# Sample rows, forget gates and first loads issued in another form in a two-layer decoder step

## The reference

```python
proj = h @ w_in                       # GLA: q, k, v, g, z; FoX: q, g
k = rms_norm(p[..., :D_B].reshape(B, L, H_B, HD_B)) * k_norm
v = p[..., D_B:2 * D_B].reshape(B, L, H_B, HD_B)
logf = jax.nn.log_sigmoid((p[..., 2 * D_B:] + b_f).astype(jnp.float32))     # 16 heads
f_all = jnp.cumsum(jnp.concatenate([logf_past, logf_new], axis=1), axis=1)
# attention: logit[t, s] = q_t . k_s / sqrt(d) + F_t - F_s  (s <= t), softmax, times v
```

## Time and profile before

| what | us |
|---|---|
| median of 3 runs (3332.48 to 3336.53) | 3336.11 |
| the profiled execution, its own time | 3337.32 |
| its span from first to last instruction | 3335.7 |
| granted TensorE clock, mean of the span | 0.923 of full speed |

### The profile page before, as it was taken

The page is one execution under the profiler, slowest core; times in us unless marked ns, Lnnn a source line. Parts: engine busy times, 40 slices in busy tenths (PEclk is TensorE's granted clock), DMA queues, the critical chain, the costliest instruction groups (busy, mean ns, idle before and its releaser), DMA issues. The chain is left out here.

```text
span 3335.7 us, 44733 instructions
## 1 busy us (share of the span) xinstructions
PE 3055.9 (92%) x16452; PEld 2203.0 (66%) x16452; DVE 1544.2 (46%) x3622; ACT 998.0 (30%) x1596; POOL 751.0 (23%) x427
## 2 busy tenths in 40 slices
PE   6589999998899968999969999889999999997799
PEld 2378787886677857888868888744444444443557
DVE  1632223211777638431137621177676767772433
ACT  0411222211555643210262211024433334433100
POOL 1310000000000002000002000247766766767000
PEclk7688989998899989999859998779999999998899
DMA  9521112212576533211032211232133213311774
GB/s 341 169 78 70 51 73 83 73 46 99 166 226 193 163 115 136 73 71 47 29 120 78 75 73 38 84 112 85 39 103 106 87 40 99 103 33 52 269 229 129
DMA packets 265625, 355.09 MB, mean 106 GB/s; under 512 B 24044, under 2 KB 156140, under 8 KB 265377
## 3 DMA queue, kind: packets, MB, share of 16 engines
q1 hardware_dynamic: 263060, 344.10, 31.0%
q0 software_dynamic: 2304, 8.39, 0.7%
q10 hardware_dynamic: 72, 0.07, 0.0%
HBM read 250.15 MB, written 102.10 MB: 106 GB/s over the span
## 5 line engine op out<-in xcount | busy, mean ns | idle before, releaser
L2210 POOL TENSOR_TENSOR at_p_sum<-at_p_sum,at_p 128x1024 f32<-128x1024 f32 (+3 forms) x264 | 541.6, 2052 | 94.5 <-ACT at_p L2066 82.8
L2066 ACT ACTIVATE at_p<-psum 128x1024 f32<-128x1024 f32 (+1 forms) x320 | 286.9, 897 | 512.8 <-PE psum L1906 510.4
L2112 DVE CUSTOM_DVE_ANT_0 psum<-psum,at_f_wide 128x512 f32<-128x512 f32 (+3 forms) x640 | 376.8, 630 | 0.0
L1986 PE MATMUL psum<-at_p,at_v 128*64 128x512 f32 (+3 forms) x1280 | 305.6, 556 | 0.1
L637 PE MATMUL psum<-kv_w_hi,kv_h_hi 128*128 128x512 f32 (+1 forms) x640 | 244.9, 383 | 17.5 <-DVE kv_h_lo L543 17.5
L638 PE MATMUL psum<-kv_w_lo,kv_h_hi 128*128 128x512 f32 (+1 forms) x640 | 244.9, 383 | 0.0
L639 PE MATMUL psum<-kv_w_hi,kv_h_lo 128*128 128x512 f32 (+1 forms) x640 | 244.9, 383 | 0.0
L974 POOL TENSOR_TENSOR kv_hs_lo<-kv_stage,kv_hs_hi 128x64 fp32r<-128x64 f32 x1 | 0.3, 320 | 1068.2 <-ACT kv_hs_hi L725 1068.2
L637 PE MATMUL psum<-gla_w_hi,gla_h_hi 128*128 128x512 f32 x512 | 201.2, 393 | 0.0
L638 PE MATMUL psum<-gla_w_lo,gla_h_hi 128*128 128x512 f32 x512 | 200.1, 391 | 0.0
L639 PE MATMUL psum<-gla_w_hi,gla_h_lo 128*128 128x512 f32 x512 | 199.9, 390 | 0.0
(11 more groups left out here) (442 smaller groups left out, 6527.5 us busy)
## 6 DMA issues: line engine op xcount, KB each, us to landing
mod_w<-in_ada_w SPq DMA_DIRECT2D x12, 2048.0 KB, 17.9
at_f_wide<-F SPq DMA_DIRECT2D x32, 512.0 KB, 5.9
at_page<-in_cache_k SPq DMA_DIRECT2D x32, 512.0 KB, 3.5
gla_w_raw<-in_gla_w_in SPq DMA_DIRECT2D x6, 2048.0 KB, 8.2
mod_w<-in_kv_ada_w SPq DMA_DIRECT2D x4, 2048.0 KB, 10.2
v_gla<-gla_stage SPq DMA_DIRECT2D x32, 256.0 KB, 2.0
sg_gla<-gla_stage SPq DMA_DIRECT2D x32, 256.0 KB, 2.0
gl_sg<-sg_gla SPq DMA_DIRECT2D x16, 512.0 KB, 4.1
```

The lines of the kernel that those rows point to most:

```text
L1986: mm = pe.matmul(bank_o[half[a], skip:NB], v[u][:, i, half[a]], p_tile[e % PT][:, a, skip:NB], start=(i == 0), stop=(i == R * G + R - 1), ...
L2066: act.activation(p_tile[e % PT][:, :, skip:NB], pair_of(bank_st[e % 2])[:, :, skip:NB], ACT.Exp)\
L2112: op = dve.tensor_tensor_reduce(pair_of(at(n))[:, a, 0:w], pair_of(at(n))[:, a, 0:w], f_wide[:, a, c * NB:c * NB + w], 1.0, -3.0e38, ALU.s ...
L2210: pool.tensor_tensor(p_sum[s][:, :, skip:NB], p_sum[s][:, :, skip:NB], p_tile[e % PT][:, :, skip:NB], ALU.add).then_inc(p_added, 1)
```

## The change

1. The sample unit of a turned block takes the form of the others (24 matmuls of 512 columns), and the 8x512 result is evacuated like theirs. Every block's sample result is stored with four DMAs of 128 columns; for a turned block each of them turns its 8x128 piece, so that its 1024 elements of 4 bytes go to separate places.
2. The `logf` block becomes `gates_products`, `gates_values`, `gates_logs` and `gates_store`: the weights stand (128 columns, 16 of them used), 512 rows stream, 4 groups of 24 matmuls; the 16 rows of the result are copied to SBUF, turned back by 16 transposes into one bank, and the gate function is made once for all 2048 rows (128x256) beside the sample (8x16). One DMA stores all rows.
3. In `kv` and `fox` group 0 of the rows is loaded and worked on ahead of the first weights.
4. `fox` runs its second headnorm block last, and the sums are made in that block.
5. The attention's first query and key rows come in four groups of two 256 KB DMAs with a signal each (`rows_first`), and each group is followed by its quarter of the running sums; the sample query and the values come after all of them.

```diff
@@ projection_phase, four new functions (shortened)
+        def gates_products(pe, three_passes):
+            for G in range(NG):
+                pe.wait_ge(evac_done, UB * n + G + 1)
+                for k in range(K):
+                    if G == 0:
+                        pe.wait_ge(w_ready, K * n + k + 1 + K)
+                    mm = three_passes(g.bank[G][:, :], (w_hi[:, k, 0:P], w_lo[:, k, 0:P]),
+                                      (h_hi[:, k, G * NB:(G + 1) * NB], h_lo[:, k, G * NB:(G + 1) * NB]), k == 0, k == K - 1)
+                mm.then_inc(ps_full, 1)
+            pe.wait_ge(evac_done, UB * n + LINES)
+            for k in range(K):
+                three_passes(g.bank[LINES][:, 0:HB], hs_rows(k), (w_hi[:, k, 0:HB], w_lo[:, k, 0:HB]),
+                             k == 0, k == K - 1).then_inc(w_free, 1)
+            for t in range(NT):
+                if t % R == 0:
+                    pe.wait_ge(gates_kept, t // R + 1)
+                mm = pe.transpose(ps_gates[:, t * HB:(t + 1) * HB], gates_T[:, t * P:(t + 1) * P], g.ident[0:HB, 0:HB])
+            mm.then_inc(gates_turned, 1)
+        def gates_values(dve):
+            for G in range(NG):
+                dve.wait_ge(ps_full, NT * n + G + 1)
+                dve.tensor_copy(gates_T[:, G * NB:(G + 1) * NB], g.bank[G][0:HB, :]).then_inc(gates_kept, 1)
+            ... # bias added to 128x256 and 8x16, absolute values, wait for gates_ln, results, copy of the sample's
+        def gates_logs(act):
+            act.wait_ge(gates_chain, 4)
+            act.activation(a_gates, a_gates, ACT.Exp, scale=-1.0).then_inc(gates_exp, 1)
+            act.activation(a_gates_s, a_gates_s, ACT.Exp, scale=-1.0).then_inc(gates_exp, 1)
+            act.wait_ge(gates_exp, 2)
+            act.activation(a_gates, a_gates, ACT.Ln, bias=g.one[:, :]).then_inc(gates_ln, 1)
+            act.activation(a_gates_s, a_gates_s, ACT.Ln, bias=g.one[0:NS, :]).then_inc(gates_ln, 1)
+        def gates_store(sp):
+            sp.wait_ge(gates_made, 1)
+            sp.dma_start(p_logf.out.rearrange("(t p) h -> p t h", p=P), g.logf_all[:, 0:W].rearrange("p (t h) -> p t h", h=HB))
+            ... # then the sample's 8x16
@@ store_units
-                    if p.turned:
-                        sp.dma_start(p.out_s[:, ds(j * c, c)], stage_s[:, 0:c]).then_inc(stored[LINES], 16)
+                    for m in range(NB // P):
+                        part_s = stage_s[0:NS, m * P:(m + 1) * P]
+                        if p.turned:
+                            dst = p.out_s[:, ds(j * (NB // P * NS) + m * NS, NS)].rearrange("p s -> s p")
+                            sp.dma_start(dst, part_s, allow_slow_non_contiguous=True).then_inc(stored[LINES], 16)
+                        else:
+                            sp.dma_start(p.out_s[:, ds(j * p.width + m * P, P)], part_s).then_inc(stored[LINES], 16)
@@ block_units
-                    if p.turned:
-                        for m in range(NB // P):
-                            for k in range(K):
-                                mm = three_passes(g.bank[LINES][:, m * NS:(m + 1) * NS], w_part,
-                                                  (hs_hi[:, k, 0:NS], hs_lo[:, k, 0:NS]), k == 0, k == K - 1)
-                                if m == NB // P - 1:
-                                    mm.then_inc(w_free, 1)
+                    for k in range(K):
+                        three_passes(g.bank[LINES][:, 0:p.width], hs_rows(k), w_part,
+                                     k == 0, k == K - 1).then_inc(w_free, 1)
@@ SP, ACT and DVE at the start of kv and fox
-                    load_w(plan[0], 0)
                     for G in range(NG):
+                        if G == 1:
+                            load_w(plan[0], 0)
                         sp.dma_start(h_lo[:, :, G * NB:(G + 1) * NB].bitcast(F32), ...)
+                    part_high(act, 0)
                 split_high(plan[0], 0)
-                    part_high(act, 0)
                     part_high(act, 1)
+                    part_values(dve, 0)
                 split_low(plan[0], 0)
-                    part_values(dve, 0)
                     part_values(dve, 1)
-                        if sums and p.base == 1:
+                        if sums and p is plan[-1]:
@@ fox_projections, plan
-                group("headnorm", w, 1, blocks - 1, ...),
-                group("silu", w, blocks, blocks, g.sg_foxT, g.sg_fox_sT, turned=True)]
+                group("silu", w, blocks, blocks, g.sg_foxT, g.sg_fox_sT, turned=True),
+                group("headnorm", w, 1, blocks - 1, ...)]
@@ attention_phase
-                load_rows(0, 0)
+                for G in range(NG):
+                    load_first_rows(G)
+                    load_f_wide(0, 0, G)
                 load_q_sample(0, 0)
-                for c in range(NG):
-                    load_f_wide(0, 0, c)
                 load_v(0, 0)
@@ turn
-                    if (a, b) == (0, 0):
+                    if isinstance(base, int) and base == 0:
+                        pe.wait_ge(rows_first[a], 32)
+                    elif (a, b) == (0, 0):
                         pe.wait_ge(rows_loaded, 32 * (2 * j + u) + 32)
```

More of the change, by code:

```diff
@@ L277, in projection_phase @@
         p.base, p.chain0, p.help0 = n, chain, helped_n
-        p.chain_per = {"headnorm": 3, "logf": 4}.get(p.kind, 0)
-        p.help_per = {"silu": 1, "headnorm": 2, "logf": 1}.get(p.kind, 0)
+        p.chain_per = {"headnorm": 3}.get(p.kind, 0)
+        p.help_per = {"silu": 1, "headnorm": 2}.get(p.kind, 0)
         n, chain, helped_n = n + p.blocks, chain + p.chain_per * UB * p.blocks, helped_n + p.help_per * UB * p.blocks
@@ L348, in projection_phase @@
             in_strip = lambda a, q: a[q * GROUP:q * GROUP + z_cols]
+        wide_logf = plan[-1].kind == "logf"
+        if wide_logf:
+            p_logf, HB = plan[-1], g.HB
+            W = NT * HB
+            gates_T, ps_gates = aux[0:HB, 0:T], g.bank[5][:, 0:W]
+            x_gates, a_gates = stage[:, 0:W], stage[:, W:2 * W]
+            x_gates_s, a_gates_s = small[0:NS, 0:HB], small[0:NS, HB:2 * HB]
+            gates_kept, gates_turned, gates_chain = sem("gates_kept"), sem("gates_turned"), sem("gates_chain")
+            gates_exp, gates_ln, gates_made, gates_stored = sem("gates_exp"), sem("gates_ln"), sem("gates_made"), sem("gates_stored")
+        full_blocks = n_blocks - wide_logf
         ps_x = [[g.bank[2 * u + b][:, :].rearrange("p (k c) -> p k c", c=P) for b in range(2)] for u in range(2)]
@@ L694, in _ @@
                 for p in plan:
-                    if p.blocks == 1:
+                    if p.kind == "logf":
+                        gates_products(pe, three_passes)
+                    elif p.blocks == 1:
                         block_units(p, 0)
@@ L764, in help_unit @@
                         act.activation(ms, ms, ACT.Sqrt, bias=g.eps[0:rows, :]).then_inc(helped, 1)
[L765 to L775, removed]
                 if turned_x is not None:
@@ L902, in _ @@
                 dve.sem_inc(evac_done, LINES)
-                for s in range(LINES + 1):
+                for s in range(LINES):
                     dve.sem_inc(stored[s], 16)
+                dve.sem_inc(stored[LINES], 64)
                 for pad in hs_pad:
@@ L927, in _ @@
                     dve.wait_ge(mask_made, 2)
+                if turned_x is not None:
+                    part_values(dve, 0)
                 split_low(plan[0], 0)
                 if turned_x is not None:
-                    part_values(dve, 0)
                     part_values(dve, 1)
@@ L948, in take @@
                         piece_end(dve, pieces)
-                block_groups(dve, plan, lambda p, j: [take(p, j, t) for t in range(NT - 1)], split_low,
-                             lambda p, j: [take(p, j, t) for t in (NT - 1, NT)])
+                block_groups(dve, plan,
+                             lambda p, j: gates_values(dve) if p.kind == "logf" else [take(p, j, t) for t in range(NT - 1)],
+                             split_low,
+                             lambda p, j: None if p.kind == "logf" else [take(p, j, t) for t in (NT - 1, NT)])
             @block.gpsimd
@@ L1719, in attention_phase @@
         rows_loaded, f_loaded = sem("rows_loaded"), sem("f_loaded")
+        rows_first = [sem(f"rows_first{G}") for G in range(NG - 1)] + [rows_loaded]
         v_loaded = [sem(f"v_loaded{u}") for u in range(2)]
@@ L1801, in load_rows, with load_first_rows @@
                             .then_inc(rows_loaded, 16)
+                def load_first_rows(G):
+                    for tile, src in zip(rows, (g.q_fox, g.k_rows)):
+                        sp.dma_start(tile[:, R * G:R * G + R, :], src.rearrange("(t p) n -> p t n", p=P)[:, R * G:R * G + R, 0:P])\
+                            .then_inc(rows_first[G], 16)
                 def load_v(j, u):
```

72 lines of the change are left out of this document (37 added, 35 removed).

## The result

The changed kernel takes 3234.51 us (median of 3 runs, 3228.38 to 3234.91) against 3336.11: a ratio of 0.9693, 95% interval [0.9671, 0.9715]. That is inside the range of 3205 to 3246, 14.5 us above the forecast of 3220, and above the 3210 to 3230 in which most of the forecast's chance lay. The profiled execution's span fell from 3335.7 to 3232.8 us, by 102.9; the forecast's sum was 115.7. So some 13 us are missing, and the question is in which term.

What follows compares the result with a forecast made beforehand. TensorE, busy 92% of the span, was taken as the bound. Savings of 49.6 + 0 + 53.6 + 8.0 + 4.5 = 115.7 us off 3337.3 made 3221.6, so a median of 3220, range 3205 to 3246.

Steps and rivals of the forecast that it cites:

- the first rival: Starts of `kv`, `fox` and attention give nothing, as DVE is late or the first quarter lands late: 3232, chance 0.18.
- 1. sample units, end of `gla` included (first two): Two turned-block sample units in `gla` fall from 18.21 and 18.19 to 5.55 us, slow starts go: 28.7 us saved.
- 1. third unit, fourth with the headnorm at `fox`'s end: In `fox`, third unit falls from 16.82 to 5.55 us, fourth nets 7.5 with headnorm last: 21.0 us saved.
- 2. turning stores, cover 30 us: Sixteen element-wise stores behind turned blocks stay hidden, with about 30 us of cover for each four: 0 lost.
- 3. `logf` block: Gates from 88.8 us to 35.2 by wide products, one chain and one store: 53.6 us won.
- 4. starts of `kv` and `fox`: Rows ahead of weights let PE start 4.8 us earlier; net 4.1 in `kv`, 3.9 in `fox`, sum 8.0.
- 5. start of the attention: Quartered first loads move everything up to the main loop 4.5 us earlier, bounds 0 to 5.5.
- the stalls at tile 5: Start of `kv`: DVE evacuates tile 1 at 1288.4 against 1287.7 wanted by tile 5, a 0.7 us stall.
- The tail: End of `fox` with the headnorm block last: 7.3 us to the next phase, against 3.27 before.
- the third, queries 1, waits for sums 0 and group 1: Attention's start: the third turn, at 2162.64 before, comes at 2158.2 once those loads land.
- The sum: Whole kernel: 115.7 us off the profiled execution's 3337.3 makes 3221.6; the median is taken as 3220.
- All four rivals: Heads give nothing 3232 (0.18); stores at 10.8 us 3273 (0.06); stores one after another 3460 (0.02); wide products half-clock 3264 (0.03).

Runs made afterwards that it cites:

- heads_back: Changed kernel with group 0 of the rows in `kv` and `fox` put behind the first weights again: 3237.8 us, ratio 0.9710 to the kernel before.
- rows_ahead: Changed kernel with each group of the attention's first rows loaded ahead of the sums of the group before it: 3228.0 us, ratio 0.9678.
- pad16: Changed kernel with 16 increments of an unused semaphore at the head of PE's list in the attention: 3226.4 us, ratio 0.9667.
- pad16_rows: Changed kernel with 16 unused semaphore increments on PE and each row group loaded ahead of the previous group's sums: 3219.7 us, ratio 0.9648.
- order_back: Changed kernel with `fox` in the old order, both headnorm blocks first and the sums in the second block: 3242.7 us, ratio 0.9720.

## Why the prediction was right, and where it was off

The direction, the range and the main terms held; one term was too large, and one assumption of the sum failed. Measured sizes are from the phases' lengths and the undone parts; parts 1 and 3 were not undone by themselves.

That the time lies in the range is in part luck. The range reached up to 3246 to take in the first rival (the heads give nothing, 3232), and 3234.5 is nearer to that rival's time than to the forecast. Yet its mechanism is refuted: *heads_back* shows 9.2 us from the heads of `kv` and `fox`. What took most of the time back is the attention's loop, which the prediction did not consider.

| step | forecast | measured |
|---|---|---|
| 1. sample units, end of `gla` included (first two) | 28.7 | 28.2 (`gla` 709.5 to 681.3) |
| 1. third unit, fourth with the headnorm at `fox`'s end | 21.0 | 21.0 (`fox` 25.85 less its head's 4.83) |
| 2. turning stores, cover 30 us | 0 | 0; 2.2 us each by sixteen |
| 3. `logf` block | 53.6 | 53.4 (`kv` 57.76 less its head's 4.35) |
| 4. starts of `kv` and `fox` | 8.0 | 9.2 |
| 5. start of the attention | 4.5 | 2.2 to 2.35 |
| the attention's loop, untouched | 0 | -12.3 in this profile |

The scan, which the sum left alone as well, gave 1.3 us; with it the rows come to some 103 us, the difference of the two spans.

**Parts 1 to 4** came out by their own steps: the units at 1.00, the block behind them without a slow start, the tail at `fox`'s end, the stalls at tile 5 (0.55 and 0.92 us against 0.7). The tail measures 6.9 us against 7.3. PE's first tile comes 4.3 us sooner in its phase in `kv` and 5.2 in `fox`, against 4.8. In the `logf` block the gates' chain takes 4.1 us (from 1628.64, the bias, to the store at 1632.72) against the 4.8 built on the earlier trace rows, store and barrier 4.3 against 3.9; from the gates' first product to `fox`'s first issue it is 34.0 us against some 35. The Trainium skill's factor for a transposing store ("DMA: Bandwidth & Descriptors", "Rules for kernel authors"), by which a store would take an estimated 26.6 us, does not show here: sixteen in 34.6 us.

**Part 5** is the mis-sized term. The step "the third, queries 1, waits for sums 0 and group 1" put that turn 4.4 us sooner; it came 2.35 sooner. *rows_ahead* shows the reason: with group 1 ahead of sums 0 the turn no longer waits for rows. The forecast named the sums in front but priced them too low.

**The sum** took the untouched loop at its old time. Its idle part, 5.9 us, is shown: a second wait at each jump, there only because 969 fewer entries ahead of the loop put its head at another place in the list (16 entries more take the wait away). Three kernels without that second wait (before, *pad16*, *pad16_rows*) have 41.1 to 41.6 us idle; the eight that jump with it have 46.4 to 48.0. The busy part, 6.35 us, goes with a lower granted clock (0.97 against 0.98) and differs between two executions of one program (803.0 and 799.8); what makes it fall behind one short wait and not behind the next stays open. All four rivals are refuted by the rows above: the heads give 9.2 us in `kv` and `fox`, the stores are cheap, and the wide products run at 1.00.

## What to carry to other kernels

A change that only shortens the code ahead of a loop can slow the loop: after any such change compare the wait behind each jump, per engine, before believing or blaming the edit. A loop of a few long turns can be worth writing out, but then on all engines that set the pace: here, with PE's alone written out, DVE's jump took the place of PE's, and the median showed next to nothing. A short loop need not be: the block loop of the projections (843 entries a turn against 2679) pays nothing for its jump. And when rows and something else share a queue, put first what the second instruction waits for, not only what the first does.

## What the hardware showed unexpectedly

- A jump back costs PE 3.4 to 4.0 us in this loop, and another 2.4 to 3.2 with the loop's head at two places in the list that lie 1024 entries apart, none at two other places, one of them only 16 entries on. That the head then lies at the end of a fetched block is inferred. The profile puts the first wait down to a DMA of data that PE does not need there; written out, it is gone. DVE's jump costs 3.25 us, ACT's 2.20.
- In the projections' block loops, with the same kind of jump, PE shows no wait at the jump, before or after. Nothing is fetched for it either: in the changed kernel's `kv` queue q8 has 4 fetches from 1410 to 1503 us, the loop's first turn, and none from 1510 to 1603, its second.

```profile
q8 instruction: 4, 0.07, 0.3%
```

- Element-wise stores of 1024 x 4 bytes go out at 2.2 us each when sixteen stand in a row; four in a row at the end of a phase make its tail 11.3 us longer than that of a headnorm block (*order_back*).
